# The pooling branch's second feature chunk made a ninth seven-block chunk that passes through DRAM

## What is computed

```python
u = rms_norm(h, norm_in_g[l])
proj = jnp.einsum('bsd,de->bse', u, w_in[l])
pool_x, pool_z, m_x, m_z = jnp.split(proj, [D_POOL, 2 * D_POOL, 2 * D_POOL + D_MLSTM], axis=-1)
# pool_x: 4 groups of 256 features; group g gets a centred moving average over 2, 4, 8 or 16 rows
pooled = jnp.stack([window_mean_minus_self(ug[:, :, g], w) for g, w in enumerate(POOL_WINDOWS)], axis=2)
mixed = jnp.einsum('bsgc,gcd->bsgd', pooled, pool_w).reshape(B, S, D_POOL)
y_pool = mixed * pool_scale * jax.nn.silu(pool_z)
```

## Time and profile before

| what | value |
|---|---|
| time, median of 3 runs | 1149.0 us (1148.96 to 1149.04) |
| time of the profiled execution | 1148.36 us |
| its span, first to last instruction | 1146.5 us |
| mean granted TensorE clock | 0.998 |
| busy share: PE, DVE, ACT, POOL | 99%, 64%, 34%, 42% |

### The profile page before, as it was taken

The page is one execution under the profiler, slowest core; times in us unless marked ns, Lnnn a source line. Parts: engine busy times, 40 slices in busy tenths (PEclk is TensorE's granted clock), DMA queues, the critical chain, the costliest instruction groups (busy, mean ns, idle before and its releaser), DMA issues.

```text
span 1146.5 us, 17447 instructions
## 1 busy us (share of the span) xinstructions
PE 1137.0 (99%) x6503; PEld 928.3 (81%) x6503; DVE 734.5 (64%) x1347; ACT 391.3 (34%) x764; POOL 476.3 (42%) x479
## 2 busy tenths in 40 slices
PE   9999999999999999999999999999999999999997
PEld 6888888888888887788888888889888887777786
DVE  5945543376944994367777965885698435555668
ACT  7432233222200123546574621341121134543322
POOL 3356656322124231344766765304233224455444
PEclk9999999999999999999999999999999999999999
DMA  8324242322355422100214231232111210142103
GB/s 246 120 65 125 96 147 93 118 98 77 121 138 203 165 101 65 57 23 25 58 38 157 94 144 56 92 125 74 55 38 50 66 62 1 39 161 90 51 35 137
DMA packets 85701, 106.17 MB, mean 93 GB/s; under 512 B 14321, under 2 KB 62665, under 8 KB 84338
## 3 DMA queue, kind: packets, MB, share of 16 engines
q1 hardware_dynamic: 77894, 101.31, 26.7%
q10 hardware_dynamic: 7724, 3.74, 1.2%
HBM read 81.40 MB, written 25.21 MB: 93 GB/s over the span
## 4 chain that ended last, share of the span: by engine, by line
PE 97%; POOL 1%; DVE 1%; issue 1%; ACT 0%; POOLq 0%; DVEq 0%; ACTq 0%
PE bank L1068 22%; PE bank L1070 21%; PE bank L1069 21%; PE bank L1372 4%; PE bank L1397 4%; PE wide L1068 3%; PE wide L1069 3%; PE wide L1070 3%; PE wide L1388 2%; PE wide L1597 2%; PE bank L1336 1%; PE bank L1325 1%; PE bank L1313 1%; PE bank L1572 1%; PE bank L1110 1%; PE wide L1572 1%
## 5 line engine op out<-in xcount | busy, mean ns | idle before, releaser
L808 POOL CAST whi<-wraw 128x2048 fp32r<-128x2048 f32 x23 | 46.1, 2006 | 330.3 <-PE bank L1070 287.1
L1068 PE MATMUL bank<-x_hi,wlo 128*128 128x512 f32 x312 | 123.5, 396 | 0.0
L1070 PE MATMUL bank<-x_hi,whi 128*128 128x512 f32 x312 | 121.6, 390 | 0.0
L1069 PE MATMUL bank<-x_lo,whi 128*128 128x512 f32 x312 | 121.5, 389 | 0.0
L1068 PE MATMUL bank<-u_hi,wlo 128*128 128x512 f32 x280 | 109.5, 391 | 0.0
L1070 PE MATMUL bank<-u_hi,whi 128*128 128x512 f32 x280 | 109.0, 389 | 0.0
L1069 PE MATMUL bank<-u_lo,whi 128*128 128x512 f32 x280 | 109.0, 389 | 0.0
L812 POOL TENSOR_TENSOR wlo<-wraw,whi 128x2048 fp32r<-128x2048 f32 x18 | 84.8, 4712 | 1.9 <-ACT whi L2922 0.5
L1068 PEld LDWEIGHTS bank<-x_hi,wlo 128*128 128x128 f32 x312 | 58.5, 188 | 16.2 <-issue 4.3
L1012 POOL TENSOR_SCALAR sp<-sp,rcx 128x384 f32<-128x384 f32 (+1 forms) x64 | 37.9, 606 | 76.4 <-DVE rcx L2409 76.4
L2322 DVE SCALAR_TENSOR_TENSOR wide<-glu,VT,wide 128x1024 f32<-128x1024 f32 x58 | 69.3, 1283 | 0.0
(11 more groups left out here) (423 smaller groups left out, 2907.8 us busy)
## 6 DMA issues: line engine op xcount, KB each, us to landing
wraw<-in_w_in SPq DMA_DIRECT2D x18, 1024.0 KB, 5.5
wraw<-in_w_out SPq DMA_DIRECT2D x12, 1024.0 KB, 5.5
wraw<-in_w_in SPq DMA_DIRECT2D x18, 512.0 KB, 4.7
xr<-in_x SPq DMA_DIRECT2D x8, 512.0 KB, 6.8
hst<-in_x SPq DMA_DIRECT2D x4, 1024.0 KB, 5.2
hpool<-hst SPq DMA_DIRECT2D x4, 1024.0 KB, 4.2
h<-hpool SPq DMA_DIRECT2D x4, 1024.0 KB, 7.1
resid<-h SPq DMA_DIRECT2D x8, 512.0 KB, 2.6
```

Of the source, the lines that this page charges most:

```text
L808: g_.tensor_copy(whi[home(w)][:, :, :], wraw[:, :, :]).then_inc(s["w_hi"], 1)
L1068: pe.matmul(ps, al, bh, start=(k == 0), stop=False)
L1069: pe.matmul(ps, ah, bl, start=False, stop=False)
L1070: return pe.matmul(ps, ah, bh, start=False, stop=(k == nk - 1))
```

## The change

The pooling branch's chunk 1 moves from place 10 to place 6 of the plan and becomes the fifth of nine seven-block chunks. Its features are summed up in `sz` like those of the others, get no Silu, and are stored to a new DRAM tensor `pxpool`. Right behind the nine chunks TensorE runs `mix(0)`, and then chunk 2. When `low_mix(0)` is done with `px`, SyncE loads chunk 1's features from DRAM into it, and `window(1, m)` waits for that load in place of ScalarE's copies. The four `pooled(1, i)` are gone. Chunk 2's low weight part is made by VectorE, where chunk 1's was before, and after `low_mix(0)` in place of ahead of it.

```diff
-    plan = [("w_in", c, "f") for c in (0, 12, 8, 9, 10, 13, 7, 6, 5, 4, 1, 2, 3)]
+    plan = [("w_in", c, "f") for c in (0, 12, 8, 9, 10, 13, 1, 7, 6, 5, 4, 2, 3)]
-SEVEN = range(2, 10)
+SEVEN = range(2, 11)
-    W_POOL, W_OP, W_MX, W_MZ, W_OM, W_2 = (0, 10, 11, 12), 13, 14, 16, 20, 24
+    W_POOL, W_OP, W_MX, W_MZ, W_OM, W_2 = (0, 6, 11, 12), 13, 14, 16, 20, 24
-    BY_VECTOR = (W_POOL[1], W_OP + 1, W_MZ + 2, W_MZ + 3, W_OM, W_OM + 1)
+    C_PX = W_POOL[1] - S0
+    BY_VECTOR = (W_POOL[2], W_OP + 1, W_MZ + 2, W_MZ + 3, W_OM, W_OM + 1)
-        return (w + (w > SEVEN[-1])) % 2
+        return w % 2
+    def px_count(g, i):
+        return 4 * (g - (g > 1)) + i + 1
+    px_d = nc.dram_tensor("pxpool", [P, 2, S], F32).ap()
...
@@ SyncE: store_7 and what follows the chunks
-                if c < 3:
+                if c < 3 or c == C_PX:
-                    dst = um_d[:, 2 * c + f, :]
+                    dst = um_d[:, 2 * c + f, :] if c < 3 else px_d[:, f, :]
...
-                        wt(W_POOL[1])
+                        wt(W_POOL[2])
                     store_7(c, f)
-            wt(W_POOL[2])
             sp_.wait_ge(s["v_px"], 3)
             mix_weights(1)
+            sp_.wait_ge(s["v_px"], 5)
+            sp_.wait_ge(s["o_st0"], 16 * (C_PX + 1))
+            sp_.wait_ge(s["o_st1"], 16 * (C_PX + 1))
+            sp_.dma_start(px[:, :, PAD:PAD + S], px_d[:, :, :]).then_inc(s["l_px"], 16)
             wt(W_POOL[3])
@@ GpSimd
-            for w in range(W_POOL[1], W_MX + 4):
+            for w in range(W_POOL[2], W_MX + 4):
                 split(w)
@@ TensorE
-            ring[0] += 1
-            for i in range(4):
-                group(W_POOL[1], i, u_hi, u_lo, "a_px", 4 + i + 1)
-                if i == 1:
-                    mix(0)
+            mix(0)
@@ VectorE
-                ve.wait_ge(s["a_px"], 4 * g + 2 * m + 2 if g else 4)
+                if g == 1:
+                    ve.wait_ge(s["l_px"], used["l_px"] + 16)
+                else:
+                    ve.wait_ge(s["a_px"], px_count(g, 2 * m + 1) if g else 4)
...
                 if c == N7 - 1:
                     ve.wait_ge(s["g_blk"], 4 * N7)
-                    low_w(W_POOL[1])
                     low_mix(0)
                 add_up(c, 4)
                 add_up(c, 5)
                 if c + 1 < N7:
                     low_last(c + 1)
+                else:
+                    low_w(W_POOL[2])
                 add_up(c, 6)
@@ ScalarE
-                if c >= 3:
+                if c >= 3 and c != C_PX:
...
-            ac.wait_ge(s["v_px"], 5)
-            for i in range(2):
-                pooled(1, i)
             for n in range(4):
                 high_y(n)
-            for i in range(2, 4):
-                pooled(1, i)
```

More of the change, by code:

```diff
@@ L391, in build @@
         l_x = [sem(f"l_x{i}") for i in range(NT)]
+        s["l_px"], used["l_px"] = s["l_g"], 16
         block = ctx.enter_context(nc.Block())
@@ L580, in store_7 @@
             def store_7(c, f):
-                if c < 3:
+                if c < 3 or c == C_PX:
                     sp_.wait_ge(s["v_sum"], 7 * c + (4, 7)[f])
-                    dst = um_d[:, 2 * c + f, :]
+                    dst = um_d[:, 2 * c + f, :] if c < 3 else px_d[:, f, :]
                 else:
-                    sp_.wait_ge(s["a_sz"], 2 * (c - 3) + f + 1)
-                    dst = sz_d[:, c - 4, f, :] if c > 3 else smz_d[:, 2 + f, :]
+                    sp_.wait_ge(s["a_sz"], 2 * (c - 3 - (c > C_PX)) + f + 1)
+                    dst = sz_d[:, c - 5, f, :] if c > C_PX else smz_d[:, 2 + f, :]
                 sp_.dma_start(dst, sz[:, f, :]).then_inc(s[f"o_st{f}"], 16)
@@ L1240, in mix @@
                     mm.then_inc(s["t_mix"], 1)
-            for i in range(4):
-                group(W_POOL[1], i, u_hi, u_lo, "a_px", 4 + i + 1)
-                if i == 1:
-                    mix(0)
+            mix(0)
             for g in (2, 3):
                 for i in range(4):
-                    group(W_POOL[g], i, u_hi, u_lo, "a_px", 4 * g + i + 1)
+                    group(W_POOL[g], i, u_hi, u_lo, "a_px", px_count(g, i))
                 mix(g - 1)
@@ L2571, in pooled @@
                 m, nh = feature_tile(W_POOL[g], i)
-                ps = filled(ac, "t_gemm", first[W_POOL[g]] + i + 1, "a_px", 4 * g + i + 1)
+                ps = filled(ac, "t_gemm", first[W_POOL[g]] + i + 1, "a_px", px_count(g, i))
                 ac.activation(px[:, m, PAD + nh * HALF:PAD + (nh + 1) * HALF], ps[:, :], ACT.Copy
```

## The result

The changed kernel takes 1151.24 us (median of 14 runs, 1149.93 to 1153.03) where the kernel before took 1149.02 (14 runs beside them, 1148.30 to 1149.61): a ratio of 1.002, with a 95% interval of 1.0013 to 1.0028. It is slower by 2.2 us, close to the bound of 0.2%. The profiled execution is one of its slower ones, 1152.53 us with a span of 1150.7, 4.2 more than that of before. Two executions of the kernel before, run beside e5 and e6, took 1426.54 and 3697.93 us, far above all others, and are left out of every median here.

A forecast was written before the change was run, and what follows sets the result against it. TensorE, busy 99% of the span, was taken to bound the kernel. Matmuls gave -2.72 us and waits for VectorE's chain +5.8, together +3.1, taking the median from 1149.0 to 1152.1 us, range 1147.5 to 1155.0.

The forecast's parts named there:

- A: Central case: VectorE's chain, held up by GpSimd, makes TensorE wait; 1152.1 us, own range 1150.6 to 1152.8, chance 0.58.
- Matmuls, -2.72: Chunk 1 as a seven-block chunk takes 84 matmuls instead of 96 on TensorE: 2.72 us less.
- rival D: One GpSimd subtraction doesn't meet VectorE's chain, at `window(2, 0)`: 1146.5 us, 1146.3 without either, chance 0.20.
- The first meeting: In `mixed(0)`, VectorE's low parts stand still for GpSimd's cast and subtraction of chunk 3's weights: cost 5.8 us.
- The second meeting: In `window(2, 0)`, VectorE stands still for GpSimd's cast and subtraction of the first output chunk: cost 6.4 us.
- rival C: First output chunk's weights take 7.7 us; cast behind the third addition, costing 2.4 less: 1149.6 us, chance 0.14.
- The wait ahead of `mix(3)`: TensorE wants `mix(3)` at 304.9, VectorE's low parts come at 308.0, start about 308.9: a wait of 4.0 us.
- The load of `px`: Chunk 1's features, reloaded on SyncE for `window(1, 0)`, cost nothing; the load would have to take 17 us.
- VectorE's end: VectorE needs 18.45 us from `mix(3)`'s low parts to freeing the second output chunk's bank: 326.5, TensorE starting at 326.6.
- The clock: TensorE's clock falling in the wait ahead of `mix(3)`: nothing in the sum, treated only as a rival, chance 0.08.
- rival B: Clock halves ahead of `mix(3)`: 5.4 us more, 1.4 hidden behind VectorE, up to 1156.1 us, chance 0.08.

The follow-up runs named there:

- e5: Kernel before the change, with ScalarE making the casts of chunk 3 and the first two output chunks: 1149.13 us, ratio 1.0002.
- e6: Changed kernel with GpSimd's cast and subtraction of chunk 3's weights cut to an eighth of their columns: 1146.45 us.
- e1: Changed kernel with ScalarE instead of GpSimd making the casts of chunk 3 and the first two output chunks: 1145.98 us.
- e4: Changed kernel with GpSimd's cast and subtraction of the first output chunk cut to an eighth of their columns: 1146.19 us.
- e3: Changed kernel with `px` loaded from DRAM twice, the second after the first has landed, `window(1, 0)` waiting for both: 1153.11 us.
- e2: Changed kernel with TensorE running the first output chunk's fourth tile twice, 12 matmuls to fill its wait: 1150.07 us.

## Why the prediction was right, and where it was off

The forecast was slower, 1152.1 us with A's own range of 1150.6 to 1152.8; the measurement is 1151.24. Step by step:

- **Matmuls, -2.72.** Right: 6491 for 6503, and e1, e4 and e6, which have no wait, are 2.4 to 3.2 us faster than before. Their 1145.98, 1146.19 and 1146.45 lie within 0.6 of the 1146.5 that rival D gave for one meeting less (e4, e6; e1 takes out the casts alone).
- **The first meeting, 5.8.** Measured 5.74. It fell one operation later than forecast, on the fourth low part and the first addition, because chunk 3's weights took 6.4 us and not 5.5. Low parts for `mix(1)`: 261.2 forecast, 261.53 measured; no wait in place of 0.2.
- **The second meeting, 6.4.** Measured 5.85, the window ending at 274.05 for 274.2. The cast went in at 265.51, behind the third addition and not the second: the load took 5.7 us for 5.2, not the 7.7 of rival C. In the order of operations it is still the case that C describes, the cast behind the third addition; but the edge waited for the cast and the closing operation for the subtraction (5.51 for 1.23), so that this order costs 5.85 and not the 4.0 (6.4 - 2.4) of C. C was priced too low. Low parts for `mix(2)`: 288.6 forecast, 288.56 measured.
- **The wait ahead of `mix(3)`, 4.0.** Measured 3.44: 307.89 for 308.0 on VectorE's side, 305.26 for 304.9 on TensorE's. The agreement of VectorE's times here and above is in part luck: in this execution the nine chunks end 0.57 late, and the chain starts from them. Counted from there it was 0.7 faster than forecast, and TensorE 0.2.
- **The load of `px`, nothing.** Right for the changed kernel. The reserve was overstated. "It would have to take 17 us" counts from a window that starts at 249.8, behind the whole first meeting; the window was ready for `px` at 245.8 in the changed kernel and, with the weights held up behind the load, at 244.3 in e3. There `px` was ready at 245.68, 13 us after the first issue, which already cost 1.9.
- **VectorE's end, 326.5.** This is the step that failed in A's central value. I let VectorE wait for the last gate load as long as before (1.59 us); it waited 0.39, as the profiled execution's row shows:

```profile
318.67 1.41 DVE L1834 SCALAR_TENSOR_TENSOR yr<-wide,VT,sz 128x512 f32<-128x512 f32 x2 [0.39 <-DMA sz<-szpool]
...
324.49 1.89 DVE L1913 TENSOR_TENSOR hst<-bank,hst 128x512 f32<-128x512 f32 x3
```

The bank was free at 324.49 + 0.65 = 325.14, 1.4 us sooner than forecast, and 1.9 when counted from the end of the nine chunks. TensorE's own side at full clock, 308.70 + 16.32 = 325.0, comes within 0.2 us of it: near the lower bound of A. In e2, where the clock stays up, VectorE's side still decides, by half a microsecond:

```profile
318.97 1.41 DVE L1837 SCALAR_TENSOR_TENSOR yr<-wide,VT,sz 128x512 f32<-128x512 f32 x2 [0.77 <-DMA sz<-szpool]
...
324.79 2.48 DVE L1916 TENSOR_TENSOR hst<-bank,hst 128x512 f32<-128x512 f32 x4
```

The bank is free at 324.79 + 0.65 = 325.44, and the second output chunk starts at 325.63 (TensorE alone: 308.61 + 16.32 = 324.93). That is 1.6 later than before when the later end of the nine chunks (0.46 here) is taken off.

- **The clock, nothing in the sum and 0.08 as rival B.** Sized too low as a chance, though not as a cost: in the profiled execution it fell as B said, over half of `mix(3)`, for 2.76 us of the 5.4 that B allowed. e2 puts its share of the median at about 1.2. The two errors partly cancel: 1.9 too much for VectorE, 1.2 too little for the clock, which leaves 0.7 of the 0.9 by which the median lies under the forecast. This is an estimate from one execution of each kernel.

So the direction and the place were right for the stated reason, which e1, e4 and e6 show by taking the meetings away in three ways, and e5 supports by showing that the same move of the casts gains nothing where the chain has reserve. That the median came within 1 us is partly luck: two errors of opposite sign. In how many of the 14 runs the clock fell can't be read without their profiles; the four above 1152 us have a mean granted clock of 0.995 or 0.996, the two lowest 0.998, but one at 1151.73 has 0.999.

## What to carry to other kernels

When matmuls are taken from the engine that sets the end, work out for each later stage how much earlier its inputs are then wanted, and whether the helper chain has that reserve: here 2.7 us of matmuls were won, and the 1146.3 us that they promised became 1151.2 because the chain behind them came into GpSimd's way. An operation of VectorE with two operands from SBUF (the on-chip memory beside PSUM) that met one of GpSimd's casts or subtractions waited here for the rest of it, even if it was 0.17 us long by itself (1.74 here, 4.45 in e1), while one with a PSUM operand kept its 0.75; before taking such work out or moving it about, look for an engine that meets nobody, as ScalarE did for the casts. A wait of a few us on TensorE should be priced with the clock that it may lose: here 3.3 us of wait, and 2.76 and 1.69 more in the two executions with that wait that were profiled.

## What the runs showed that was not expected

In the profiled execution of the changed kernel a pause of 3.3 us was enough for the granted clock to read 0.50 by its end; it stayed there through the first 13 of `mix(3)`'s matmuls (0.427 us apart for 0.2267), which took 2.76 us longer. Some 0.3 of this is hidden: at full clock TensorE would have waited for VectorE's banks instead. In e3 a pause of the same length ahead of `mix(3)` left the clock at 1.00 up to its end, near 310, and the fall came after it:

```profile
308.00:310.00 2.00, 0.00 (x0) 0.00 (x0) 2.00 (x3) 0.00 (x0) 0.00 (x0) 1.00 0.02 4
310.00:312.00 2.00, 1.73 (x4) 1.49 (x5) 1.93 (x4) 1.26 (x2) 0.00 (x0) 0.56 0.44 116
312.00:314.00 2.00, 2.00 (x7) 1.55 (x7) 1.96 (x4) 0.92 (x2) 0.00 (x0) 0.59 1.05 407
```

There `mix(3)` took 317.40 - 310.27 = 7.13 us, 1.69 more than its 5.44. So the same pause did not cost the same twice. Pauses of 0.6 us in e2 and of 1.4 us in e3, ahead of `mix(1)`, left the clock at 1.00.

The ten matmuls at the start of the program took between 5.00 and 6.53 us in eight profiled executions, at a granted clock of 1.00 in all of them, and the nine chunks ended between 234.10 and 234.91 in the six executions that were profiled with nine. Differences of a few tenths between spans mean nothing until this is taken off.
